# Delta rule of a hybrid block: inversion levels one to five as pairs of 64-row matmuls, one bank for each half

## What is computed

```python
decay = exp(where(incl, gcum[..., :, None] - gcum[..., None, :], -inf))
k_beta = k * beta[..., None]
a_strict = where(strict, einsum('bhcik,bhcjk->bhcij', k_beta, k) * decay, 0.0)
rhs = concatenate([v * beta[..., None], k_beta * exp(gcum)[..., None]], axis=-1)
sol = triangular_solve(a_strict, rhs, left_side=True, lower=True, unit_diagonal=True)
```

## Time and profile before

| | us |
|---|---|
| median of 3 runs | 3269.26 |
| lowest, highest | 3268.76, 3269.83 |
| the profiled execution, its own time | 3268.28 |
| its span, first to last instruction | 3266.5 |
| TensorE products, busy | 3174.3 (97%) |
| TensorE weight loads, busy | 3007.6 (92%) |
| VectorE, busy | 1980.8 (61%) |
| ScalarE, busy | 1390.2 (43%) |
| GpSimd, busy | 183.5 (6%) |

### The profile page before, as it was taken

The page is one execution under the profiler, slowest core; times in us unless marked ns, Lnnn a source line. Parts: engine busy times, 40 slices in busy tenths (PEclk is TensorE's granted clock), DMA queues, the critical chain, the costliest instruction groups (busy, mean ns, idle before and its releaser), DMA issues.

```text
span 3266.5 us, 63194 instructions
## 1 busy us (share of the span) xinstructions
PE 3174.3 (97%) x25502; PEld 3007.6 (92%) x25502; DVE 1980.8 (61%) x2587; ACT 1390.2 (43%) x1742; POOL 183.5 (6%) x273
## 2 busy tenths in 40 slices
PE   6899999999998999999999999999999999999999
PEld 1588888888887899999999999999999999999999
DVE  6666666665767866665555555556666555555544
ACT  5534443444443544444433333344444443333333
POOL 0000000000001000011100000010001110000000
PEclk9999999999999999999999999999999999999999
DMA  9611111111229544455555555554444555555554
GB/s 347 245 65 51 64 64 64 51 64 65 78 91 357 187 178 179 168 180 193 193 193 193 193 193 193 193 218 170 178 171 177 193 193 193 193 193 193 193 193 154
DMA packets 79878, 543.64 MB, mean 166 GB/s; under 512 B 8325, under 2 KB 12437, under 8 KB 15264
## 3 DMA queue, kind: packets, MB, share of 16 engines
q1 hardware_dynamic: 74064, 514.88, 42.6%
q10 hardware_dynamic: 4976, 23.85, 2.0%
q0 software_dynamic: 736, 3.46, 0.3%
HBM read 537.94 MB, written 4.22 MB: 166 GB/s over the span
## 4 chain that ended last, share of the span: by engine, by line
PE 87%; DVE 5%; issue 4%; ACT 2%; DMA 1%; PEld 0%; DVEq 0%; ACTq 0%; POOLq 0%; PEldq 0%; POOL 0%
PE bank L400 25%; PE bank L401 25%; PE bank L402 25%; PE bank L594 5%; DVE w_lo L384 1%; ACT w_hi L379 1%; DMA gate_raw<-stream 1%; PE bank L600 1%; PE bank L635 1%; PE bank L644 1%; DVE g_acc L1360 1%; DVE s_acc L1360 0%; PE bank L916 0%; PE bank L726 0%; DVE gate_acc L1712 0%
## 5 line engine op out<-in xcount | busy, mean ns | idle before, releaser
L384 DVE TENSOR_TENSOR w_lo<-raw,w_hi 128x2048 fp32r<-128x2048 f32 x477 | 1095.4, 2297 | 588.6 <-ACT w_hi L379 588.6
L379 ACT CAST w_hi<-raw 128x2048 fp32r<-128x2048 f32 x477 | 911.6, 1912 | 1270.3 <-PE bank L402 1236.5
L400 PE MATMUL bank<-a_lo,w_hi 128*128 128x256 f32 (+1 forms) x3664 | 1085.0, 296 | 14.6 <-DVE w_lo L384 6.7
L401 PE MATMUL bank<-a_hi,w_lo 128*128 128x256 f32 (+1 forms) x3664 | 1068.5, 292 | 0.0
L402 PE MATMUL bank<-a_hi,w_hi 128*128 128x256 f32 (+1 forms) x3664 | 1068.3, 292 | 0.0
L400 PE MATMUL bank<-h_lo,w_hi 128*128 128x256 f32 x3584 | 1000.9, 279 | 0.5
L401 PE MATMUL bank<-h_hi,w_lo 128*128 128x256 f32 x3584 | 990.4, 276 | 0.0
L402 PE MATMUL bank<-h_hi,w_hi 128*128 128x256 f32 x3584 | 990.2, 276 | 0.0
L400 PEld LDWEIGHTS bank<-a_lo,w_hi 128*128 128x128 f32 x3664 | 693.0, 189 | 34.8 <-DVE w_lo L384 7.6
L402 PEld LDWEIGHTS bank<-a_hi,w_hi 128*128 128x128 f32 x3664 | 692.2, 189 | 19.8
L401 PEld LDWEIGHTS bank<-a_hi,w_lo 128*128 128x128 f32 x3664 | 693.6, 189 | 17.6
(11 more groups left out here) (310 smaller groups left out, 2200.8 us busy)
## 6 DMA issues: line engine op xcount, KB each, us to landing
raw<-stream SPq DMA_DIRECT2D x485, 1024.0 KB, 4.8
gate_raw<-stream ACTq DMA_DIRECT2D x16, 1024.0 KB, 5.4
xr<-x_t SPq DMA_DIRECT2D x4, 1024.0 KB, 16.5
turned<-by_distance POOLq DMA_DIRECT2D x1, 2048.0 KB, 14.7
x_res<-x_t ACTq DMA_DIRECT2D x1, 2048.0 KB, 20.3
bias_table<-bias ACTq DMA_DIRECT2D x1, 2048.0 KB, 9.6
bias<-bias_table ACTq DMA_DIRECT2D x1, 2048.0 KB, 9.4
out_t<-x_res SPq DMA_DIRECT2D x4, 512.0 KB, 5.1
```

Of the source, the lines that this page charges most:

```text
L379: act.copy(w_hi[u.slot][:], raw[u.raw][:]).then_inc(hi_ready, 1)
L384: dve.tensor_tensor(w_lo[u.slot][:], raw[u.raw][:], w_hi[u.slot][:], ALU.subtract).then_inc(lo_ready, 1)
L400: pe.matmul(acc, wh, lo[:, k, 0:n], start=(k == first), stop=False)
L401: pe.matmul(acc, wl, hi[:, k, 0:n], start=False, stop=False)
```

## The change

At levels 1 to 5 each matmul of a chunk becomes two that contract over 64 rows: rows 0 to 63 for the left 64 columns, rows 64 to 127 for the right 64. The first writes to bank 4 + 2d, the second to bank 5 + 2d, for X and for the second product alike, and at level 5 for the "old" product too (at column 128). Streamed columns for each of the two are 64 for X and 32 for the second product. Level 6 keeps its form, in banks 4 + 2d (X) and 5 + 2d. ScalarE copies each result in two instructions of 128 columns, one from each bank (`from_rows`); VectorE masks X with one instruction that reads both banks of a direction, which for that are allocated as pairs.

```diff
-        psum = [ctx.enter_context(nc.psum_tensor(f"bank{k}", [P, 512], F32)) for k in range(8)]
+        psum = [ctx.enter_context(nc.psum_tensor(f"bank{k}", [P, 512], F32)) for k in range(4)]
+        pairs_of_banks = [ctx.enter_context(nc.psum_tensor(f"bank{k}", [P, 1024], F32)) for k in (4, 6)]
+        psum += [b[:, k * 512:(k + 1) * 512] for b in pairs_of_banks for k in range(2)]
...
+            def by_rows(d, at, products):
+
+                for n, (lhs, *rhs) in enumerate(products):
+                    for h in range(2):
+                        r, w = slice(h * 64, h * 64 + 64), math.prod(rhs[h].shape[1:])
+                        last = mm(psum[4 + 2 * d + h][:, at + n * w:at + (n + 1) * w], lhs[r], rhs[h][r], start=True, stop=True)
+                return last
+
+            def halves_of(stationary, moving, level, d, which):
+
+                return [(lhs, half_blocks(x[:, 0:64], level, d, which), half_blocks(x[:, 64:P], level, d, which))
+                        for lhs, x in zip(stationary, moving)]
...
-                        each(4 + d, zip(blocks(g_L, d), blocks(g_U, d))).then_inc(S["x_mm"], 1)
+                        if level < 6:
+                            m = by_rows(d, 0, [(l, u[:, 0:64], u[:, 64:P]) for l, u in zip(blocks(g_L, d), blocks(g_U, d))])
+                        else:
+                            m = each(4 + 2 * d, zip(blocks(g_L, d), blocks(g_U, d)))
+                        m.then_inc(S["x_mm"], 1)
...
-                        m = each(6 + d, [(t, half_blocks(x, level, d, "new")) for t, x in zip(blocks(g_T, d), blocks(g_X, d))], w=64)
+                        if level < 6:
+                            m = by_rows(d, 0, halves_of(blocks(g_T, d), blocks(g_X, d), level, d, "new"))
+                        else:
+                            m = each(5 + 2 * d, [(t, half_blocks(x, level, d, "new"))
+                                                 for t, x in zip(blocks(g_T, d), blocks(g_X, d))], w=64)
                         if level == 5:
-                            m = each(2 + d, [(x, half_blocks(t, level, d, "old"))
-                                             for t, x in zip(blocks(g_T, d), blocks(g_X, d))], w=64)
+                            m = by_rows(d, P, halves_of(blocks(g_X, d), blocks(g_T, d), level, d, "old"))
...
+            def from_rows(out, d, at, level, which):
+
+                w, k = 1 << level, int((d == 0) == (which == "new"))
+                for h in range(2):
+                    to = out.rearrange("p (n h m two w) -> p n h m two w", n=4, h=2, two=2, w=w)[:, :, h, :, k]
+                    m = act.copy(to, psum[4 + 2 * d + h][:, at:at + P].rearrange("p (n m w) -> p n m w", n=4, w=w))
+                return m
...
-                        m = act.copy(half_blocks(g_U[:, half], level, d, "new"), d3(psum[6 + d][:, 0:L], 1 << level))
+                        if level == 6:
+                            m = act.copy(half_blocks(g_U[:, half], level, d, "new"), d3(psum[5 + 2 * d][:, 0:L], 1 << level))
+                        else:
+                            m = from_rows(g_U[:, half], d, 0, level, "new")
                         if level == 5:
-                            m = act.copy(half_blocks(g_T[:, half], level, d, "old"), d3(psum[2 + d][:, 0:L], 1 << level))
+                            m = from_rows(g_T[:, half], d, P, level, "old")
...
-                        tt(half3(g_X, d), d3(psum[4 + d][:], P), over(K("level", (1 - d) * LEVELS + level), 4), ALU.mult
-                           ).then_inc(S["xp_ready"], 1)
+                        mask = K("level", (1 - d) * LEVELS + level)
+                        if level < 6:
+                            m = tt(g_X[:, d * 512:d * 512 + 512].rearrange("p (n h w) -> p h n w", n=4, h=2),
+                                   d3(pairs_of_banks[d][:], 512)[:, :, 0:L].rearrange("p h (n w) -> p h n w", n=4),
+                                   d3(mask, 64).unsqueeze(2).broadcast_to([P, 2, 4, 64]), ALU.mult)
+                        else:
+                            m = tt(half3(g_X, d), d3(psum[4 + 2 * d][:], P), over(mask, 4), ALU.mult)
+                        m.then_inc(S["xp_ready"], 1)
```

## The result

The changed kernel takes 3307.51 us (median of 4 runs, 3301.95 to 3323.86) against 3269.55 us for the kernel before in the same measurement (4 runs, 3268.76 to 3273.96). The ratio is 1.0122, interval 1.0085 to 1.0158: about 38 us slower. The direction was forecast; 3280.7 us and the range up to 3300 were too low. The profiled execution took 3307.45 us, with a span of 3305.3 us against 3266.5 before.

The account below looks back on a forecast made before the run. TensorE's products were taken to bound the kernel. Switches of 14.9 us less 3.5 us from pace gave +11.4 us, so 3280.7 us from a median of 3269.26; the 8-in-10 range was 3271 to 3300 us.

Parts of the forecast that it names:

- What sets the step: Delta-rule levels: loading 128 weight columns sets 0.1115 us a step; two half products together cost what one full product cost.
- Pace 0.109: Levels 1 to 5: 64-row steps at 0.109 us instead of 0.1115, gaining 3.5 us over 1408 steps.
- Switches: Six 64-row stretches per head: 0.20 us entering, 0.11 leaving, 14.9 us over eight heads (9.6 to 19.2).
- Copies, mask, banks: ScalarE's split copies, VectorE's two-bank mask and shared banks: cost 0; copies at level 5 at most 2.8 us.
- The step that failed: Delta-rule stretch: TensorE read as running at the granted full clock, 2.4 GHz; no clock term in the sum.
- TensorE was fed: Rival, TensorE cannot be fed: four instructions per step at 0.036 us each, +49 us, some 3330 us; chance 0.10.
- Halves in series: Rival, levels 1 to 5: halves run one after the other, +153 us, 3434 us; chance 0.02.
- the quicker load: Rival, levels 1 to 5: half loads take less, steps fall towards 0.055 us, 3207 us; chance 0.07.
- Nearly nothing: Rival: leaving 64-row stretches almost free, steps at 0.107 us, +3.3 us, 3272.6 us; chance 0.14.

Follow-up runs that it names:

- the second profile: The unmodified change measured again, against the kernel before: 3306.87 us, ratio 1.0079; its profiled execution took 3309.05 us.
- the diagonal form: The change with 64x64 weights at levels 1 to 5 and TensorE's head loop written out, against the kernel before: 3228.94 us (0.9869), again 3260.52 us (0.9891).

## Why the prediction was wrong in size

Its direction and the mechanism that it named stood; a second one, larger, was missing.

- **What sets the step.** Forecast: the load of 128 weight columns, not shortened. Right. The steps keep 0.11 us; in series they would be twice that (7.09 us for 64 products); with 64 weight columns they halve (0.058). The Trainium skill, "TensorE: Matmul & The Clock Gate", LDWEIGHTS, says that the time of a load goes by its columns and not its rows; the traces agree, 188 ns at 64x128, 192 at 128x128, 134 at 64x64.
- **Pace 0.109.** Wrong: it was the row of another form, in which each load has 64 weight columns. The 3.5 us that it took off are not there.
- **Switches.** 0.31 us a pair forecast, 0.32 measured (4.04 against 3.72), though split as 0.15 in and 0.17 out, not 0.20 and 0.11. Six stretches and eight heads make 0.32 x 48 = 15.4 us; by the head without a fall it is (73.86 - 71.80) x 8 = 16.5, against 14.9 forecast. The Trainium skill, "TensorEngine Tiling (Array Packing)", Key Properties, says that a change of mode drains TensorE; the traces agree, with a gap at every change, and give its price, also after last products as short as 32 columns.
- **Copies, mask, banks: nothing.** Right; the copies were tried alone (ratio 0.9998).
- **The step that failed** is one that the prediction reads and doesn't question: TensorE works "at the granted full clock (2.4 GHz) through the delta-rule stretch". That holds for the kernel before; the sum took it as given for the changed kernel and put the clock at nothing without a reason. The term that is missing is the clock: 16 falls x 1.5 us = 24 us. With it, 16.5 + 24 = 40.5 us, which is what the delta rule grew by (640.0 - 599.5); in the second profile it is 16.5 + 10 x 1.5 = 31.5 us against 31.9 measured. Without it, the time would have been 3269.5 + 16.5 = 3286 us, inside the range and within the forecast's own 3275 to 3291.
- **Rivals.** TensorE was fed: pairs start every 0.11 us, and every 0.058 us in the diagonal form. Halves in series and the quicker load fell with the steps. "Nearly nothing" fell with the way out, which isn't cheaper after a short last product, and with the steps, which stay at 0.11 us.

What is shown: the falls are there in the change, go when the same 64-row products stream twice the columns, come with 128 rows as well when each load is followed by 32 or 64 columns, and become fewer, and come at other places, when part of the products is made full again. What is argued only: which quantity the chip looks at. The diagonal form streams as few columns for each load as the change and has no fall; its steps take half the time, its runs are shorter (2.3 us from first to last product where the change takes 3.5), and they have a wait for a copy inside. Which of these saves it was not tried apart. Nor was it settled why a head has sometimes one fall and sometimes two, or which of its runs they follow.

## What to carry to other kernels

Before splitting a contraction to use both halves of TensorE's rows, see whether the load or the streaming sets the step: where the load does, halve the weight columns too (a block-diagonal operand allows it: 41 us faster here), or leave it. Count each meeting of 64-row and 128-row products at 0.3 to 0.4 us the pair, and keep products of one form together. And do not carry the granted clock of the trace before over to the changed kernel: fewer columns for each load, at the same step, can cost the clock without a single idle gap, so read it by stretches afterwards.

## What was not expected of the hardware

- The granted clock fell to 1.2 GHz while TensorE showed no idle time at all (6.00 of 6.00 us, 6.50 of 6.50 us busy ahead of the falls), for 3.4 us each time in the change. The Trainium skill, "TensorE: Matmul & The Clock Gate", Part 1, has the clock follow how busy TensorE has been; the runs here agree only if busy is not what the busy row of a profile shows.
- Streaming twice the columns made a kernel faster, 3291.03 against 3307.51 us, since they were free under the loads and kept the clock up.
- With 128 weight columns, leaving the 64-row form takes 0.20 us from the last product's start to the next product's, after 32, 64 or 128 streamed columns alike; with 64 weight columns it takes 0.15.
- The Trainium skill, "TensorEngine Tiling (Array Packing)", Theoretical Speedup, promises up to twice the speed for contractions of at most 64. With 128 weight columns it was 1.2% slower for the kernel; only with 64 weight columns as well did the steps halve.
